# Local attention and the first block of the recurrence, one after the other or interleaved

## The reference

```python
p_a, p_q, p_k, p_v, p_c = jnp.split(p, split_pts, axis=-1)
y_a, v_first = rwkv7_mixer(p_a, v_first, ...)        # recurrence: 6 heads of 64, state 64 x 64
y_b = chunk_attention(p_q, p_k, p_v, ...)            # local attention: 6 heads of 64
y_c = multiscale_pool(p_c, ...)                      # trailing means minus the token, then a small matrix
x = x + jnp.concatenate([y_a, y_b, y_c], axis=-1) @ w_out[l]
```

## Time and profile before

| | us |
|---|---|
| median of 3 runs (2620.62 to 2631.18) | 2627.58 |
| the profiled execution | 2626.4 |
| its span | 2624.6 |
| PE busy / DVE busy / ACT busy in the span | 2305.2 (88%) / 1069.0 (41%) / 857.3 (33%) |

### The profile page before, as it was taken

How to read it: one execution, slowest core, us unless ns; L and a number is a source line. 1 busy time by engine, 2 the same in 40 slices (tenths; PEclk the granted TensorE clock), 3 DMA queues, 4 the chain that set the end, 5 groups by cost and what they waited for, 6 DMA issues and landing times.

```text
span 2624.6 us, 37287 instructions
## 1 busy us (share of the span) xinstructions
PE 2305.2 (88%) x15288; PEld 1641.8 (63%) x15288; DVE 1069.0 (41%) x1681; ACT 857.3 (33%) x1348; POOL 77.0 (3%) x87
## 2 busy tenths in 40 slices
PE   7998998677787777776779999899999999899999
PEld 7996593233333333222238888788888889778887
DVE  7767761000000000000025467565555547555544
ACT  4483140000010000000034455355445445445543
POOL 0000012000000000000000001000000000200000
PEclk9999999888887888889889999999999999899999
DMA  6434089999999999999986543144556554023553
GB/s 244 173 135 144 2 337 392 427 427 427 427 427 427 427 426 427 427 427 427 427 339 216 192 166 115 35 161 136 186 192 202 191 192 153 33 99 117 187 190 115
DMA packets 116818, 669.15 MB, mean 255 GB/s; under 512 B 10826, under 2 KB 14069, under 8 KB 56400
## 3 DMA queue, kind: packets, MB, share of 16 engines
q1 hardware_dynamic: 111376, 650.14, 63.7%
q0 software_dynamic: 3008, 12.96, 1.4%
q10 hardware_dynamic: 2304, 4.20, 0.4%
HBM read 662.01 MB, written 5.24 MB: 254 GB/s over the span
## 4 chain that ended last, share of the span: by engine, by line
PE 56%; DMA 25%; SPq 5%; DVE 5%; issue 3%; ACT 2%; DVEq 2%; POOLq 1%; ACTq 0%; POOL 0%
PE psd L641 22%; PE psd L635 10%; PE psx L641 9%; DMA scr<-in_w_up 8%; DMA ring<-in_w_down 7%; DMA hx<-in_w_down 6%; SPq L3032 5%; DMA e_w_hi<-in_w_up 2%; PE psd L1044 1%; DVE scr L2083 1%; PE psx L1059 1%; PE psd L1006 1%; PE psx L1300 1%; DMA ring<-in_w_gate 1%; PE psx L885 1%
## 5 line engine op out<-in xcount | busy, mean ns | idle before, releaser
L2083 DVE TENSOR_TENSOR w_lo<-ring,w_hi 128x1024 fp32r<-128x1024 f32 x436 | 515.8, 1221 | 392.2 <-ACT w_hi L1543 391.3
L1543 ACT ACTIVATE w_hi<-ring 128x1024 fp32r<-128x1024 f32 x436 | 437.0, 1048 | 474.8 <-PE psd L641 248.7
L641 PE MATMUL psd<-w_hi,h_cut 128*128 128x512 f32 x1536 | 481.4, 395 | 3.9 <-DVE h_cut L2083 3.5
L635 PE MATMUL psd<-h_cut,w_hi 128*128 128x256 f32 x1824 | 337.3, 287 | 12.1 <-DVE h_cut L2083 7.8
L641 PEld LDWEIGHTS psd<-w_hi,h_cut 128*128 128x128 f32 x1536 | 284.2, 188 | 61.5 <-DVE h_cut L2083 4.4
L641 PE MATMUL psd<-w_lo,h_cut 128*128 128x512 f32 x768 | 300.2, 391 | 0.0
L635 PEld LDWEIGHTS psd<-h_cut,w_hi 128*128 128x128 f32 x1824 | 288.0, 194 | 16.6 <-issue 13.9
L635 PE MATMUL psd<-h_cut,w_lo 128*128 128x256 f32 x912 | 260.1, 285 | 0.0
L641 PE MATMUL psx<-w_hi,halves 128*128 128x512 f32 x704 | 218.0, 391 | 0.0
L1532 ACT ACTIVATE scr<-psd 128x512 f32<-128x512 f32 x48 | 28.6, 596 | 566.3 <-PE psd L1022 359.4
L2083 DVE TENSOR_TENSOR scr<-psd,scr 128x512 f32<-128x512 f32 x20 | 13.8, 690 | 435.4 <-PE psd L1006 435.3
(11 more groups left out here) (391 smaller groups left out, 2901.0 us busy)
## 6 DMA issues: line engine op xcount, KB each, us to landing
ring<-in_ffn_wi SPq DMA_DIRECT2D x88, 1024.0 KB, 5.3
scr<-in_w_gate SPq DMA_DIRECT2D x48, 1024.0 KB, 26.6
scr<-in_w_down SPq DMA_DIRECT2D x48, 1024.0 KB, 26.2
scr<-in_w_up SPq DMA_DIRECT2D x48, 1024.0 KB, 26.9
ring<-in_ffn_wo SPq DMA_DIRECT2D x44, 1024.0 KB, 4.9
ring<-in_w_gate SPq DMA_DIRECT2D x32, 1024.0 KB, 26.6
ring<-in_w_up SPq DMA_DIRECT2D x32, 1024.0 KB, 27.0
ring<-in_w_down SPq DMA_DIRECT2D x32, 1024.0 KB, 26.5
```

The source lines that it names most:

```text
L635: mm = pe.matmul(o, w[u], a[:, v, :], start=start and i == 0, stop=stop and i == 2, **kw)
L641: mm = pe.matmul(o, a[:, u, :], w[v], start=start and i == 0, stop=stop and i == 2)
L1543: act.activation(hi, src, ACT.Copy).then_inc(hi_cut, 1)
L2083: return dve.tensor_tensor(o, a, b, op)
```

## The change

The attention's steps are taken apart and put between the steps of block 0 of the recurrence on TensorE, DVE and ACT. For that the attention's products go to the `psd` banks with a semaphore of their own (`attention_done`), and its tiles move: `prob`, the kept values (`v_att_of`), `share`, and block 0's CT, DT and WU lie in the weight parts `w_hi`/`w_lo` of the last two `mix_in` slots, `probT` in `hx`. `kt` and `rt` are made ahead of everything else. The bonus product and what follows from it (bonus, gating, `mix_rest`) go to the end of block 0. No arithmetic is added or dropped, and block 1 is as it was, but that the copy of its turned `be` is made earlier.

```diff
+def attention_banks(early):
+    if early:
+        return [("av_tr", 0, "act"), ("av_tr", 1, "act"), ("score", 0, "dve"), ("score", 1, "dve"), ("score", 2, "dve"),
+                ("prob_tr", 0, "act"), ("score", 3, "dve"), ("prob_tr", 1, "act"), ("score", 4, "dve"),
+                ("prob_tr", 2, "act"), ("score", 5, "dve"), ("prob_tr", 3, "act")]
+    return [("prob_tr", 4, "act"), ("prob_tr", 5, "act"), ("att", 0, "act"), ("att", 1, "act"), ("att", 2, "act"),
+            ("pool", 0, "act"), ("att_share", 0, "dve"), ("att_share", 1, "dve")]
...
+        plan += [((part, l, i), reader) for part, i, reader in attention_banks(True)]
+        plan += [((("state", l), i), "dve") for i in range(4)]
+        plan += [((part, l, i), reader) for part, i, reader in attention_banks(False)]
+        plan += [((("state", l), i), "dve") for i in range(4, STATES)]
...
@@ TensorE @@
-                turned(0, "abkv")
+                turned(0, "ab")
+                pe.wait_ge(S("qk_ready"), l + 1)
+                score(0)
...
                     pair("AT", be, al)
+                        score(1)
+                        turned(0, "kv")
                     mats("P2", "AT", mat("A"), wait=after("A", "AT"))
                     mats("P2T", "A", mat("AT"))
                     pair("BT", kt, al)
+                        score(2)
...
+                        prob_back(0)
+                        score(3)
                         pe.wait_ge(S("rw_scaled"), 4 * l + 4)
                     pair("CT", be, rt, P)
                     mats("Q4", "P4", mat("Q"), wait=after("P4", "Q2"))
                     mats("P8", "P4T", mat("P4"), wait=after("P4T"))
+                        prob_back(1)
                     pair("DT", kt, rt, P)
+                        score(4)
                     mats("Q8", "P2", mat("Q"), wait=after("P8", "Q4"))
...
                     mats("X1", "Aoff", mat("Q"))
+                        prob_back(2)
+                        score(5)
...
                     mats("Q32", "P2T", mat("P4"), wait=after("TR", "X1"))
-                        pe.wait_ge(S("rk_ready"), l + 1)
-                        for i in range(2):
-                            b = m2(XB.claim(pe, ("bonus", l, 0, i)))
...
+                        prob_back(3)
...
                         for g, name in ((1, "b"), (2, "k"), (3, "v")):
                             turned(1, name)
                             state_step(g)
+                            if g < 3:
+                                prob_back(3 + g)
+                        for q in range(HP):
+                            attended(q)
+                        pooled()
+                        shares()
+                        pe.wait_ge(S("rk_ready"), l + 1)
+                        for i in range(2):
+                            b = m2(XB.claim(pe, ("bonus", l, 0, i)))
...
                         b = from_chunks()
@@ ScalarE @@
+                solved(0, "P2", "P2T")
+                score_exp(0)
+                solved(0, "P4", "P4T")
+                prob_kept(0)
+                score_exp(1)
+                solved(0, "P8")
+                prob_kept(1)
+                score_exp(2)
+                solved(0, "TR", "X1")
+                prob_kept(2)
+                solved(0, "BV")
+                score_exp(3)
+                prob_kept(3)
+                solved(0, "WU")
+                turned(1, "a")
+                score_exp(4)
+                score_exp(5)
+                turned(1, "k")
+                prob_kept(4)
+                turned(1, "v")
+                prob_kept(5)
+                attention_kept()
+                cutter.upto(slot_of((("mix_out", l), 0)))
+                from_chunks(0)
+                cutter.upto(slot_of((("mix_out", l), 1)))
@@ VectorE, in block 0 @@
+                tt_(kt[:, :, :], k_, e2, ALU.mult).then_inc(S("rw_scaled"), 1)
+                tt_(rt[:, :, :], r_, e1, ALU.mult).then_inc(S("rw_scaled"), 1)
...
+                        scored(0)
                     masked(tt, "BT")
                     add_to_q(tt, "Q2")
+                        scored(1)
                     masked(tt, "CT", P)
                     add_to_q(tt, "Q4")
+                        scored(2)
                     masked(tt, "DT", P)
                     add_to_q(tt, "Q8")
+                        scored(3)
+                        scored(4)
                     add_to_q(tt, "Q32")
+                        scored(5)
...
+                        dve.wait_ge(S("pooled"), l + 1)
+                        state(0)
+                        shares_spread()
+                        for g in range(1, 4):
+                            state(g)
+                        keys_turned(1)
+                        attention_scaled()
+                        bonus()
+                        bonus_gated()
+                        dve.wait_ge(S("mix_rest_hi"), l + 1)
+                        tt_(h_lo[:, 3:8, :], ycat[:, 3:8, :], h_hi[:, 3:8, :].bitcast(F32),
+                            ALU.subtract).then_inc(S("mix_rest"), 1)
```

More of the change, by code:

```diff
@@ L303, in small_plan @@
                 add("act", "vup", l, i)
-        add("act", "av_tr", l, 0)
-        add("act", "av_tr", l, 1)
-        for step in range(8):
-            if step < 6:
-                add("dve", "score", l, step)
-            if step > 1:
-                add("act", "prob_tr", l, step - 2)
-        for q in range(HP):
-            add("act", "att", l, q)
-        add("act", "pool", l)
-        for tt in range(TT):
-            add("dve", "att_share", l, tt)
         def turned(tt, names):
@@ L338, in small_plan @@
                 turned(1, "bkv")
+                for i in range(2):
+                    add("dve", "bonus", l, 0, i)
             add("act", "Y", l, tt)
@@ L456, in x_ready, with a_ready @@
             return XB.bank(key)
+        ATTENTION = {}
+        for l in range(LAYERS):
+            for early in (True, False):
+                for part, i, _ in attention_banks(early):
+                    ATTENTION[part, l, i] = len(ATTENTION) + 1
+        def a_ready(eng, *key):
+            eng.wait_ge(S("attention_done"), ATTENTION[key])
+            return DB.bank(key)
         PAIRS = pair_order()
@@ L1944, in _, with a_read @@
                                 j = 2 * n + m
-                                ins = act.activation(v_gate[:, j, :], b[:, m, :], ACT.Sigmoid, bias=pc("a_v0", j))
+                                ins = act.activation(v_gate_of(l)[:, j, :], b[:, m, :], ACT.Sigmoid, bias=pc("a_v0", j))
                             read(ins)
-                for tt in range(TT):
-                    b = x_ready(act, "av_tr", l, tt)
-                    read(copy(v_tm[:, tt, :], b[:, 0:AW]))
+                def a_read(ins):
+                    ins.then_inc(d_read["act"], 1)
                 def score_exp(hd):
@@ L2003, in gn_root, with solved @@
                                         scale=1.0 / 64))
-                for x_ in "akv":
-                    turned(0, x_)
-                for tt in range(TT):
-                    for name, dst in (("P2", "P2"), ("P2T", "P2T"), ("P4", "P4"), ("P4T", "P4T"), ("P8", "P2"),
-                                      ("TR", "P2T"), ("X1", "P4"), ("BV", None), ("WU", "WU")):
-                        if tt and name == "P4":
-                            gn_square(0)
-                        if tt and name == "P8":
-                            gn_root(0)
+                def solved(tt, *names):
+                    MATS = mats_of(l, tt)
+                    for name in names:
+                        dst = {"P8": "P2", "TR": "P2T", "X1": "P4"}.get(name, name)
                         for p in range(2):
@@ L2020, in _ @@
                                 read(copy(MATS[dst][p][:, :, :], tri(b, P if name == "WU" else 64)))
[L2021 to L2030 removed]
+                for x_ in "akv":
+                    turned(0, x_)
+                solved(0, "P2", "P2T")
[23 more added lines that the diff above has]
+                cutter.upto(slot_of((("mix_out", l), 1)))
+                solved(1, "P2", "P2T")
+                gn_square(0)
+                solved(1, "P4", "P4T")
+                gn_root(0)
+                solved(1, "P8", "TR", "X1", "BV", "WU")
+                from_chunks(1)
                 def mix_hi(tt):
@@ L2751, in add_to_q @@
                         b = tri(x_ready(dve, name, l, tt, p), 64)
[L2752 removed]
+                        read(tt_(square_mats["Q"][p], b, square_mats["Q"][p], ALU.add))
                 def state(g):
@@ L2848, in _ @@
                     else:
-                        bonus()
+                        scored(5)
+                        for j in range(HP):
+                            ins = dve.scalar_tensor_tensor(out=bonus_in[:, j, :], in0=r_[:, j, :],
+                                                           scalar=pc(f"a_r_k{l}", j), in1=k_[:, j, :], op0=ALU.mult,
+                                                           op1=ALU.mult)
```

(1 more changed line is left out.)

238 lines of the change are left out of this document (131 added, 107 removed).

## The result

The changed kernel took 2603.62 us (median of 4 runs, 2599.7 to 2607.75), the kernel before on the same chip 2625.9 (4 runs); the ratio is 0.9919, 95% interval 0.9905 to 0.9933. Run again later it was 2603.71 (6 runs), ratio 0.9927 (0.9915 to 0.9939). The forecast was 2608. The profiled executions took 2626.4 and 2607.75 us, 18.65 apart.

The account below looks back on a forecast made before the run. No engine is full; a chain of hand-offs bounds the mixer. Gains of 11.1 (layer 0) and 9.9 (layer 1), less 0.8 table load and 0.5 hand-offs, give 19.7 us: 2606.7 profiled, 2608 median; range 2602 to 2614.

Parts of the forecast that it names:

- TensorE's work: Merged stretch, per layer: attention's 10.5 us at full clock plus block 0's own 27.5, 38.0 in all, the stretch's floor.
- TR: Block 0: TensorE still waits 0.69 us for Q8's addition on DVE, as before.
- Ahead of `prob_back(3)`: In front of WU: a new TensorE idle of about 1.0 us, waiting for exp 3 on ACT.
- M 0.7: Block 0 behind WU: the TensorE wait of 0.67 us in front of M stays.
- States: State steps of block 0: 0.45 us of TensorE's short waits stay; shares_spread between state 0 and 1 costs nothing.
- Tail: End of the stretch: DVE's scaling, bonus, gating and mix_rest take 6.3 us after the shares, making DVE 1.5 us late.
- Layer 1: ACT's table load of 1.28 us stands in front of the copies of P4 and P4T, with 0.5 us room: 0.8 lost.
- Nothing is lost: Start of the stretch: kt and rt on DVE ahead of A's mask are covered by 2.3 us of TensorE work; no cost.
- rival C: Clock falls in the merged stretch: up to 38.0 us more per layer, 2684 us if low throughout; chance 0.07.
- what this stretch loses the kernel loses: Everything before and after the merged stretch keeps its order, so its 11.1 and 9.9 us gains pass to the whole.
- A (heads in the path): scored(0) to scored(3) delay block 0's additions and masks: 6.2 us per layer come back, 2620.5 us; chance 0.17.
- D (all waits close): TensorE's waits close wholly but for the tail: stretch 39.5 us, 2.9 per layer less, about 2602; chance 0.08.

Follow-up runs that it names:

- three small edits: Changed kernel with mix_rest moved into block 1, prob_back(3) behind WU and al's turn, GpSimd held until kt and rt are made: 2599.77 us, ratio 0.9903.
- idle turns: The kernel before, with 15 and 6 extra turns of the queries into a free bank where TensorE waits in attention: 2624.77 us, ratio 0.9991.

## Why the prediction was right

It put the gain into 42.4 us a layer for the merged stretch; measured are 41.4 and 42.6. Its milestones, in us from the first turned value (layer 0):

| | forecast | measured |
|---|---|---|
| A, P2, CT | 2.3, 4.9, 10.6 | 2.3, 4.9, 10.4 |
| Q8, WU, M | 14.9, 21.6, 24.2 | 15.5, 22.2, 24.9 |
| shares done | 36.1 | 35.6 |
| first mask of block 1 | 42.4 | 41.4 |

- **TensorE's work**, 38.0: measured 38.48. The sum is right by luck: two terms missed in opposite directions. A head's scores cost 0.85 us from start to start (1631.00 to 1631.85), where 0.52 was taken from the row of 12 in 1.57: six heads are 2.0 more. That row is three heads in a row, and their instructions overlap: up to six are in progress in the same 0.05 us, at most three of a head that stands alone. The row comes again with 1.57 in both layers of both profiles of the kernel before, at full clock. The price of a head alone stood in the trace before as well, at full clock in layer 1 (the next group starts at 2262.56, 0.85 later):

```profile
2261.71 0.92 PE L1171 MATMUL psx<-scr 64*128 64x128 f32 x4
```

  Even and odd heads lie in different halves of the 128 rows (`r = 64 * (hd % 2)`), which would let neighbours run at once; no run varied that. Interleaving puts other work between the heads and gives this overlap up. Attention's part came to 12.3 (0.7 values, 5.0 scores, 2.8 turns back, 2.1 values times probabilities, 1.0 pool, 0.7 shares, from start to start) and not 10.5, so block 0's own was 26.2 and not 27.5. That the rows of block 0 held ends of groups that stood before a wait, which cost nothing when work follows at once, is an explanation and was not tested.
- **Idle**, 4.4 in all: measured 2.9. TR 0.7: measured 0.16. Head 4's scores stand between DT and Q8 on TensorE, so VectorE's mask of DT ended 0.3 us ahead of Q8's products, and not 0.2 us behind them as before. Ahead of `prob_back(3)` 1.0: measured 0.71, at the place and from the engine named; moving it gave 1.05. M 0.7: 0.67. States 0.45: 0.45. Tail 1.5: 0.9 (0.31 for a bank, some 0.6 until the mask), and VectorE's chain from the shares on was 6.0 us, forecast 6.3; taking `mix_rest` out of it gave 1.4 in the stretch, 0.4 of it for good.
- **Layer 1** was forecast 0.8 us longer, for the table load. It is 1.2 longer, and not for that. The load stands where it was put, between the copies of P2T and P4, but CT begins 11.6 us in against 10.4 in layer 0, and P2 already 6.1 against 4.9: nothing is added across the load. With GpSimd held back both layers take 41.32, with the load still there. The failed step is "kt and rt now run on DVE (0.96 each) ahead of the mask of A" with its "Nothing is lost": beside GpSimd they took 3.44. The Trainium skill (SBUF — State Buffer, "Who interferes with whom") says that a VectorE instruction with two SBUF inputs contends with a GpSimd instruction that reads SBUF; the trace agrees that they contend. The same section calls the ports that they share an exclusive lock, where issue order decides who blocks; here both lengthened, GpSimd's from 1.81 to 2.63.
- The Trainium skill's 2.66 us for a table switch (ScalarE: Activation LUTs, "What ACT_TABLE_LOAD costs") is not borne out by the rows: load at 2254.85, exp at 2256.15, 1.30 us; the load itself, 1.28, agrees.
- **The clock** stayed at 1.00 in both stretches in both profiles (rival C did not come). It did not in two kernels built from this one (0.95 without attention, 0.96 in layer 1 with AT three times), so it is no sure thing. The prediction's own mark for being wrong, more than 3 us lost or won outside the stretch, was just passed in the profiled pair: 3.2 lost, 2.3 of them in block 1. That "what this stretch loses the kernel loses" failed there. By the medians 22.3 us were gained for the stretches' 21.8, and the second profiles of the two kernels, on two chips, are 22.9 apart with 22.1 in the stretches: no loss outside shows there.
- **Rivals.** A (heads in the path) would have made the stretches 6.2 us longer: no wait of TensorE over 0.16 us stands behind `scored(0)` to `scored(2)`, and they end at 41.4. D (all waits close) gave 39.5 for the stretch; three small edits reach 38.9, so these waits were there to be closed, but not by this change.
- **The whole** came out at 2603.6 and not 2608: by the medians the gain was 22.3 and not 19.7 us, 2.1 of that difference in the stretches (21.8), and the kernel before stood 1.7 lower than in the runs shown first (2625.9 and 2627.6).

## What to carry to other kernels

Two chains of short hand-offs that each leave TensorE idle are worth running through each other, and the gain can be laid out beforehand: sum TensorE's work from start to start of its groups, then place the other engines' pieces and count only what comes last. Look then at the first and the last operation of the merged stretch and at what the idle engines (here GpSimd) do at that moment: there stood 2.65 of the 3.7 us that three small edits then took from layer 1's stretch. Measure also what such an edit does behind the stretch: `mix_rest` gave 1.4 us there and took 1.0 back in block 1. Price a group from a row where it stands as it will stand after the change: three heads' scores in a row cost 0.52 us each, one alone 0.85. Two kernels here filled TensorE's waits with dummy work in the hope of the clock, and neither was clearly faster for it.

## What the runs showed of the hardware

**VectorE and GpSimd slow each other.** Two float32 products of 128x768 from SBUF to SBUF took 1.82 us on VectorE with GpSimd held back, 2.23 in layer 0 and 3.44 in layer 1 beside it; GpSimd's addition 1.81 held back and 2.63 beside them.

**Half clock wanders from kernel to kernel.** Half-clock time around the two mixers (as defined in the expectation of the kernel before's second profile) was 40.9, 44.4 and 50.1 us with attention in front, and 17.0 to 27.3 in eight profiles of kernels with attention interleaved; with idle turns 23.8 and 34.1. In the changed kernel it fell in block 1 in both layers of both profiles, and TensorE is busy throughout. Busy time by window, layer 0:

```profile
1672.00:1674.00 2.00, 2.00 (x40) 1.88 (x40) 1.77 (x7) 0.53 (x2) 0.00 (x0) 0.72 0.00 0
1674.00:1676.00 2.00, 2.00 (x55) 2.00 (x53) 0.71 (x2) 1.20 (x4) 0.00 (x0) 0.50 0.00 0
```

It comes right behind a wait of 1.34 us, but the kernels with GpSimd or `prob_back(3)` moved were at 1.00 there (32.8 us for block 1). What else decides it stays open.

**TensorE can stand where the profile shows nothing that holds it.** In the kernel with idle turns TensorE stood for 2.47 and 2.75 us at the same matmul of layer 1's block 1, in two profiles of two. TensorE's row in the second:

```profile
2326.21 0.33 PE L1416 MATMUL psx<-scr,hx 128*64 128x128 f32 x2 [2.75 <-issue]
```

"issue" means that nothing in the profile held it. The DMA view of 2322 to 2327 us of that kernel (busy tenths and GB/s in 40 slices of 0.125 us, then the queue that carries instructions: packets, MB, share) has

```profile
GB/s 197 524 459 328 590 197 590 393 328 590 131 0 0 0 0 131 0 0 0 0 0 0 0 0 0 0 0 0 0 0 0 0 0 0 0 0 0 0 0 0
...
q8 instruction: 1, 0.02, 1.2%
```

A weight slot's transfer ends at 2323.4, one block of instructions follows at 2323.9, and TensorE goes on 2.2 us after it, with the clock at half behind. The stand of 1.62 us in the kernel with AT made three times (layer 1) and that of 1.71 in the one without attention (layer 0) end some 2.5 us behind such a block as well, with no weights near. The kernel before has one in layer 0's stretch too, of 0.82 and 1.10 us in its two profiles. The changed kernel has one of 0.81 around its mixers, in block 1 of layer 1 of its first profile, and none of 0.5 or more in the merged stretches. The Trainium skill (Runtime: NRT & Kernel Launch, "Instruction fetch mechanics") calls the cost of crossing a block of instructions mostly hidden; if these stands are that cost, it is not always hidden in these dense stretches of small matmuls. That they come from the fetch is read from the times of these rows; no run here varied it.
